# Splitting the 256-token products of the dense gate and up into two of 128 tokens, in a two-layer hybrid attention and MoE block

## The reference, cut to what matters

```python
def swiglu(h, wg, wu, wd):
    return (jax.nn.silu(h @ wg) * (h @ wu)) @ wd

for layer in range(DEPTH):                     # DEPTH = 2
    h = h + hybrid_mixer(rms_norm(h, attn_norm[layer]), ...)
    hn = rms_norm(h, ffn_norm[layer])
    if layer % 2 == 0:
        h = h + swiglu(hn, dense_w_gate[j], dense_w_up[j], dense_w_down[j])
    else:
        h = h + moe_ffn(hn, ...)
return rms_norm(h, final_norm)
```

## Time and profile before

| | us |
|---|---|
| median of 2 runs | 1544.29 |
| their range | 1543.68 to 1544.90 |
| the profiled execution | 1545.17 |
| its span, first to last instruction | 1543.3 |
| mean granted TensorE clock | 0.985 |

### The profile page before, as it was taken

The page is one execution under the profiler, slowest core; times in us unless marked ns, Lnnn a source line. Parts: engine busy times, 40 slices in busy tenths (PEclk is TensorE's granted clock), DMA queues, the critical chain, the costliest instruction groups (busy, mean ns, idle before and its releaser), DMA issues.

```text
span 1543.3 us, 19978 instructions
## 1 busy us (share of the span) xinstructions
PE 1506.9 (98%) x7674; PEld 1274.5 (83%) x7674; DVE 1263.1 (82%) x1564; ACT 1034.1 (67%) x1332; POOL 73.1 (5%) x148
## 2 busy tenths in 40 slices
PE   8989999999999999999999999999999999999996
PEld 7877899999787788888888888888888888888885
DVE  6587555655558789999899999899899899999995
ACT  6464544444355367887787787787788787778784
POOL 4220000000213000000000000000000000000000
PEclk9999999999998799999999999999999999999999
DMA  7511645554342149999999999999999999999992
GB/s 292 199 56 55 238 165 204 178 184 154 123 160 94 56 155 372 380 366 376 356 356 374 352 359 378 348 366 377 354 363 378 343 373 356 372 365 377 368 367 99
DMA packets 181825, 431.68 MB, mean 280 GB/s; under 512 B 3808, under 2 KB 10336, under 8 KB 181728
## 3 DMA queue, kind: packets, MB, share of 16 engines
q1 hardware_dynamic: 180720, 428.01, 75.4%
q10 hardware_dynamic: 1008, 2.36, 0.4%
HBM read 429.31 MB, written 1.05 MB: 279 GB/s over the span
## 4 chain that ended last, share of the span: by engine, by line
PE 88%; DVE 6%; ACT 2%; DMA 2%; issue 1%; POOL 1%; DVEq 0%; POOLq 0%; ACTq 0%; SPq 0%
PE pair L874 39%; PE work L874 31%; PE pair L1050 9%; PE work L846 2%; PE pair L940 2%; PE pair L846 2%; DVE w_lo L1546 1%; DMA ring<-in_moe_w_down 1%; PE work L861 1%; PE work L1015 1%; PE work L1135 1%; DVE hn L1538 0%; DVE arena L1605 0%; DVE nmax L1636 0%; PE work L1149 0%
## 5 line engine op out<-in xcount | busy, mean ns | idle before, releaser
L1546 DVE TENSOR_TENSOR w_lo<-ring,w_hi 128x1024 fp32r<-128x1024 f32 (+3 forms) x810 | 963.6, 1215 | 190.2 <-ACT w_hi L1234 177.0
L1234 ACT ACTIVATE w_hi<-ring 128x1024 fp32r<-128x1024 f32 (+3 forms) x810 | 841.0, 1053 | 317.9 <-PE work L874 100.1
L874 PE MATMUL work<-w_hi,hidT_hi 128*128 128x512 f32 x504 | 197.0, 391 | 1.7 <-DVE hidT_lo L1797 1.7
L874 PE MATMUL work<-w_lo,hidT_hi 128*128 128x512 f32 x504 | 196.2, 389 | 0.0
L874 PE MATMUL work<-w_hi,hidT_lo 128*128 128x512 f32 x504 | 196.1, 389 | 0.0
L874 PE MATMUL pair<-w_hi,hnT_hi 128*128 128x512 f32 x480 | 189.7, 395 | 2.4 <-DVE hnT_lo L1554 1.5
L874 PE MATMUL pair<-w_hi,hnT_lo 128*128 128x512 f32 x480 | 187.2, 390 | 0.0
L874 PE MATMUL pair<-w_lo,hnT_hi 128*128 128x512 f32 x480 | 186.8, 389 | 0.0
L874 PE MATMUL pair<-w_hi,xU_hi 128*128 128x512 f32 x448 | 177.1, 395 | 0.0
L874 PE MATMUL pair<-w_hi,xU_lo 128*128 128x512 f32 x448 | 174.8, 390 | 0.0
L874 PE MATMUL pair<-w_lo,xU_hi 128*128 128x512 f32 x448 | 174.3, 389 | 0.0
(11 more groups left out here) (230 smaller groups left out, 1911.5 us busy)
## 6 DMA issues: line engine op xcount, KB each, us to landing
ring<-in_moe_w_gate SPq DMA_DIRECT2D x56, 2048.0 KB, 9.6
ring<-in_moe_w_up SPq DMA_DIRECT2D x56, 2048.0 KB, 10.2
ring<-in_moe_w_down SPq DMA_DIRECT2D x56, 2048.0 KB, 9.4
ring<-in_dense_w_gate SPq DMA_DIRECT2D x7, 2048.0 KB, 7.5
ring<-in_dense_w_up SPq DMA_DIRECT2D x7, 2048.0 KB, 7.6
ring<-in_dense_w_down SPq DMA_DIRECT2D x7, 2048.0 KB, 7.8
ring<-in_w_in SPq DMA_DIRECT2D x4, 2048.0 KB, 8.8
ring<-in_w_out SPq DMA_DIRECT2D x4, 2048.0 KB, 9.5
```

The source lines that it names most:

```text
L874: mm = pe.matmul(b, lhs[x_part][k + kk], w[w_part][:, kk, :], start=(first and kk == 0 and i == 0), stop=(last and kk == 1 and i == 2))
L1234: return act.activation(o, i, ACT.Copy)
L1546: dve.tensor_tensor(lo, raw, hi.bitcast(F32), ALU.subtract).then_inc(lo_done, 1)
```

## The change

Inside `columns_turned` the token dimension of each product is split: for each stationary weight block and each of the three pairs of parts, a matmul for tokens 0 to 127 and one for tokens 128 to 255 follow each other, each writing its half of the region. `start` is set on the very first of them for a bank, `stop` on the very last.

```diff
@@ -1045,10 +1045,13 @@
                     w = part_buffers(part + i, 512)
                     for kk in range(2):
                         for f in range(4):
-                            b = banks[f // 2][:, f % 2 * S:f % 2 * S + S]
                             for n, (x_part, w_part) in enumerate(((0, 0), (0, 1), (1, 0))):
-                                mm = pe.matmul(b, w[w_part][:, kk, f * P:(f + 1) * P], (hnT_hi, hnT_lo)[x_part][:, 2 * i + kk, :],
-                                               start=((i, kk, f % 2, n) == (0, 0, 0, 0)), stop=((i, kk, f % 2, n) == (3, 1, 1, 2)))
+                                for t in range(T):
+                                    b = banks[f // 2][:, f % 2 * S + t * P:f % 2 * S + t * P + P]
+                                    mm = pe.matmul(b, w[w_part][:, kk, f * P:(f + 1) * P],
+                                                   (hnT_hi, hnT_lo)[x_part][:, 2 * i + kk, tile(t)],
+                                                   start=((i, kk, f % 2, n, t) == (0, 0, 0, 0, 0)),
+                                                   stop=((i, kk, f % 2, n, t) == (3, 1, 1, 2, T - 1)))
                     mm.then_inc(part_used, 1)
```

## The result

The changed kernel takes 1665.0 us (1664.4 to 1665.6) where the kernel before took 1544.29: 1.0782 times as long, 95% interval 1.0735 to 1.0828, 120.7 us more. The forecast was 1662, with a range from 1652 to 1686.

A forecast was written before the change was run, and what follows sets the result against it. PE was taken to bound the dense stage: 2304 products x 111 ns = 255.7 us, less 138.2 us, is 117.5 us more on 1545.17, so 1662.7, median 1662 us; range 1652 to 1686.

The forecast's parts named there:

- The bound: Dense stage: PE runs without a gap, so time added per product is added to the end; nothing changes before the stage.
- Two loads for two products: Dense gate and up: each product keeps its own weight load, so 1152 products and 1152 loads are added.
- The rival with both halves hidden: Dense gate and up: both halves hide their loads, 133 ns in place of 120 per pair, 1560 us; chance 5%.
- the middle case: Dense gate and up: one load at the floor, one free, 178 ns per pair, 66.8 us more, 1611 us; chance 5%.
- The price of a 128-wide product: Dense gate and up: 111 ns per load and product, between 107 and 120, 117.5 us more; chance 84%.
- The three rows that it rested on: Earlier trace: two 130-column products (112 ns each), eight 128-column transposes (110) and 32 products of 8 columns (109).
- the debt of 15 to 20 ns behind the 130-wide pair: At L1173: slower 512-wide products behind the pair; if that time belongs to the pair, its price is 120 ns, the upper end.
- The guess for the lower end: Dense gate and up: 107 ns per product, as if a load took twice as long per column as a product; 1652.6 us.
- The rule weighed: The skill's 81 ns per load and 128-column product would give 186.6 us in gate and up, some 1593 us; not followed.
- By columns alone 67 ns: Price of a 128-wide gate or up product from its moved columns alone: 128 x 0.42 + 13 = 67 ns.
- The rival of the clock: Dense gate and up: granted clock falls to 0.50, 213 ns per product, 352.5 us more, 1897 us; chance 3%.
- Narrow products at a price that doesn't fall: Dense gate and up: each narrow product costs up to 0.227 us, 385 us more, 1929 us; chance 2%.

The follow-up runs named there:

- the run with gate alone: Against the kernel before, only the gate products were split into two 128-wide ones, up stayed at 256 columns; 1606.6 us, ratio 1.0418.
- the run with the other order: Against the changed kernel, only the order differs: all three products of one 128-token tile, then the three of the other; 1664.3 us, ratio 1.0762.
- half the load: Against the changed kernel, each gate and up product loads 64 of 128 weight columns and writes 64 partitions, still moving 128 columns; 1548.0 us, ratio 1.0003.
- the quarters: Against the kernel before, each 256-wide gate and up product became four of 64 columns with full loads; 2377.2 us, ratio 1.537.
- the three products: Against the kernel before, each 256-wide gate and up product became three of 128, 64 and 64 columns, full loads; 2137.4 us, ratio 1.381.

## Why the prediction was right

*The bound.* Right: PE alone carried the dense stage, before and after; the dense stage became 119.23 us longer, which L1051 and the down blocks account for, and the run with gate alone shows that each half of it counts. The attention stages on both sides moved by 4.55 and -4.45 us, together with their granted clock, which the prediction had at nothing; that this cancelled was luck.

*Two loads for two products.* Right: 2304 loads at L1051, and the run with the other order, with a third of the repeats, has the same time, so a repeated load is neither dropped nor shorter. One sentence of the prediction is not shown as it stands, that a product can't start before its own block is loaded: in the earlier trace rows the record of a product starts at 652.61 us and that of its load lasts from 652.55 to 652.74. What the runs show is the price of the two together. The rival with both halves hidden (1560) and the middle case (1611) are out.

*The price of a 128-wide product.* 111 was taken, 111.5 measured; the 0.5 ns x 2304 are 1.2 us of the 1.7 us by which the profiled execution differs from its forecast (1664.4 against 1662.7), the rest is in the down blocks. The three rows that it rested on, were short (2, 8 and 32 products) and agreed with each other and with the long stream. For the transposes of the earlier trace rows that agreement doesn't show what it was taken for. The kernel before has transposes that load 96 columns and move 128:

```profile
53.30 1.48 PE L846 MATMUL work<-ident,arena 128*96 128x128 f32 x12
54.62 0.61 PE L940 MATMUL pair<-arena 98*128 98x128 f32 x4
```

From 53.30 to 54.62 that is 110 ns for each of the 12, as with 128 loaded columns, though 96 x 0.83 + 5 would be 85. So the price of these plain float32 transposes didn't fall with the load, what sets it is open, and the earlier trace rows is no evidence for the load, though its number came out right. The weight lies on the earlier trace rows. The price of 120 that the debt of 15 to 20 ns behind the 130-wide pair allowed for is out: such a debt isn't paid per product. The down blocks after 384 halves are 0.08 us longer; whether that is such a debt isn't shown.

*What the floor is.* The prediction laid it on the load; that was argued there, and half the load shows it, with the reserve that the written partitions are halved too: 111.5 ns becomes 60.0 beside 128 moved columns, and 58.3 beside 64. The guess for the lower end, a load that takes twice as long per column as a product, would come to 0.83 ns per column against 0.42 with 5 ns on top, if 58.3 is the floor of the half load.

*The rule weighed.* The about 81 ns of the Trainium skill (TensorE: Matmul & The Clock Gate, Back-to-back issue gap) don't hold for these float32r products with full loads; 111.5 does. The same page of the Trainium skill, under LDWEIGHTS, gives a load of P columns as about P / 1.2 ns, 107 for 128; the measured 111.5 and 58.3 lie 5 ns above that line at 128 and 64.

*The part that was mis-sized.* "By columns alone 67 ns": 60.0 with half loads. The some 13 ns that don't depend on the moved columns do depend on the load: they are 6.7 at 64 and at 32 loaded columns. It moved nothing in the forecast, since a full load was made anyway.

*The rival of the clock.* It didn't come in this kernel, but the argument against it was weak. The stream of 8-wide products in the earlier trace rows lasted 3.5 us at a granted 1.00, and the quarters show that such a stretch proves nothing: they too ran at the full level for 3 us, and the three products for 5.7 us, before the clock fell to 0.50. The price written for the rival, 213 ns per product, is what both runs at the lower level show (61.28 / 288 = 212.8 ns with three products). The two halves kept granted 1.00 over blocks of 42.8 us; three products (128, 64 and 64 columns) or four of 64 in their place did not, and four of 64 with half loads did. What decides between these runs stays open: they differ in the load, the written partitions and the distance between starts.

*Narrow products at a price that doesn't fall.* Out: 60.0 ns for 128 columns with a small load, and 192 and 64 columns together cost what 128 and 128 do.

## What to carry to other kernels

In a stream of float32r products each of which loads its own block, the price of one in these runs is the larger of what its moved columns take and what its load takes; for 128 loaded columns the second is 111.5 ns, so that 256 moved columns (119.9 ns) hide the load with little to spare, and 192, 128 and 64 all pay for it. Splitting 512 columns into two of 256 costs some 13 ns, splitting 256 into two of 128 costs 103, nearly a whole load; the price is read from the distance between starts in rows that move few columns, never from the length of a record. A row of another kind of product, as the plain float32 transposes, can give the same number for another reason; it is worth looking for one that varies the supposed cause. And a stream in which PE never waits can still lose the full clock, as those of three and four products for each former one did, which a row of a few microseconds doesn't rule out.

## What was not expected of the hardware

The extra beside the moved columns takes two values in these runs: about 13 ns at 128 loaded columns (227 for 512 moved, 119.9 for 256), and 6.7 at 64 and at 32 (113.4 for 256 moved, 60.0 for 128). The clock fell to 0.50 in stretches where PE never waited, for 64-wide products 111 ns apart with full loads, and not for products of the same width 58 ns apart with half loads. Transposes in plain float32 cost 110 ns with 96 loaded columns and with 128.
